# A decoder step on one core: the output projection with LN1, and the last FFN group with LN3, each ordered by token chunks

## The reference

```python
h = x @ w_in + b_in; a, g, p = jnp.split(h, [D_CONV, 2 * D_CONV], axis=-1)
u = a * jax.nn.sigmoid(g)                       # causal depthwise conv, width 31, group norm, silu
mix = jnp.concatenate([o_conv, o_pool], axis=-1) @ w_out
x = layer_norm(DN_ALPHA * x + mix, ln1_g, ln1_b)
x = layer_norm(DN_ALPHA * x + cross_attn(x, mem_k, mem_v, xq_w, xo_w), ln2_g, ln2_b)
f = jnp.square(jax.nn.relu(x @ w1 + b1)) @ w2 + b2
x = layer_norm(DN_ALPHA * x + f, ln3_g, ln3_b)
```

## Time and profile before

| | |
|---|---|
| median of 3 runs | 1454.04 us (1453.9 to 1457.93) |
| the profiled execution: its own time, its span | 1453.77 us, 1451.9 us |
| PE busy | 1374.4 us, 95% of the span, 8454 matmuls |
| DVE, POOL, ACT busy | 780.2, 671.3, 346.3 us |
| mean granted clock of PE | 0.976 |

### The profile page before, as it was taken

The page is one execution under the profiler, slowest core; times in us unless marked ns, Lnnn a source line. Parts: engine busy times, 40 slices in busy tenths (PEclk is TensorE's granted clock), DMA queues, the critical chain, the costliest instruction groups (busy, mean ns, idle before and its releaser), DMA issues.

```text
span 1451.9 us, 20585 instructions
## 1 busy us (share of the span) xinstructions
PE 1374.4 (95%) x8454; PEld 1317.0 (91%) x8454; DVE 780.2 (54%) x848; ACT 346.3 (24%) x659; POOL 671.3 (46%) x392
## 2 busy tenths in 40 slices
PE   7999889997899979999999999999999999999994
PEld 6999877696699968889999999999999999999993
DVE  4899998379712652477773115531154311454568
ACT  4222441212711431135320002200022100221114
POOL 3377986136752704539533333333333333343470
PEclk9999999998999989999999999999999999999997
DMA  8222432001011066301111111111111111111103
GB/s 249 61 48 80 120 131 73 15 29 30 15 44 44 6 230 231 129 17 37 37 44 55 47 44 44 43 44 43 45 53 48 44 44 43 44 44 45 43 15 119
DMA packets 44382, 93.52 MB, mean 64 GB/s; under 512 B 20256, under 2 KB 26656, under 8 KB 41888
## 3 DMA queue, kind: packets, MB, share of 16 engines
q1 hardware_dynamic: 34560, 89.73, 19.5%
q10 hardware_dynamic: 9760, 2.93, 0.8%
HBM read 85.39 MB, written 7.25 MB: 64 GB/s over the span
## 4 chain that ended last, share of the span: by engine, by line
PE 70%; DVE 19%; POOL 6%; issue 2%; ACT 2%; DMA 1%; SPq 0%; DVEq 0%; ACTq 0%; POOLq 0%
PE bank L589 22%; PE bank L590 21%; PE bank L591 21%; DVE conv_sum L1474 10%; POOL x_low L504 1%; DVE conv_sum L1483 1%; DVE x_full L1619 1%; ACT x_full L1270 1%; POOL x_full L349 1%; POOL w_low L340 1%; PE conv_sum L751 1%; DVE bank L1629 1%; DVE x_low L1461 1%; DMA dec_kv<-dec_kv_in 1%; DVE x_full L1636 1%
## 5 line engine op out<-in xcount | busy, mean ns | idle before, releaser
L589 PE MATMUL bank<-x_high,w_high 128*128 128x384 f32 (+1 forms) x1200 | 391.6, 326 | 15.2 <-POOL w_low L340 11.8
L338 POOL TENSOR_TENSOR w_high<-w_raw,ones 128x1024 fp32r<-128x1024 f32 x84 | 163.0, 1940 | 514.8 <-PE bank L591 255.3
L590 PE MATMUL bank<-x_low,w_high 128*128 128x384 f32 (+1 forms) x1200 | 388.6, 324 | 0.0
L591 PE MATMUL bank<-x_high,w_low 128*128 128x384 f32 (+1 forms) x1200 | 387.9, 323 | 0.0
L589 PE MATMUL bank<-mix,w_high 128*128 128x384 f32 (+1 forms) x1024 | 335.9, 328 | 7.3 <-DVE x_full L1726 2.8
L590 PE MATMUL bank<-mix,w_high 128*128 128x384 f32 (+1 forms) x1024 | 335.0, 327 | 0.0
L591 PE MATMUL bank<-mix,w_low 128*128 128x384 f32 (+1 forms) x1024 | 332.1, 324 | 0.0
L589 PEld LDWEIGHTS bank<-x_high,w_high 128*128 128x128 f32 x1200 | 226.1, 188 | 18.4 <-POOL w_low L340 11.2
L591 PEld LDWEIGHTS bank<-x_high,w_low 128*128 128x128 f32 x1200 | 226.4, 189 | 0.0
L590 PEld LDWEIGHTS bank<-x_low,w_high 128*128 128x128 f32 x1200 | 226.3, 189 | 0.0
L340 POOL TENSOR_TENSOR w_low<-w_raw,w_high 128x1024 fp32r<-128x1024 f32 x84 | 211.7, 2520 | 6.6
(11 more groups left out here) (244 smaller groups left out, 1687.7 us busy)
## 6 DMA issues: line engine op xcount, KB each, us to landing
w_raw<-slabs_in SPq DMA_DIRECT2D x110, 512.0 KB, 3.5
dec_kv<-dec_kv_in SPq DMA_DIRECT2D x16, 1024.0 KB, 5.4
scratch<-slabs_in SPq DMA_DIRECT2D x8, 512.0 KB, 3.6
yT_res<-x_full SPq DMA_DIRECT2D x4, 768.0 KB, 3.5
x_full<-xT_in SPq DMA_DIRECT2D x4, 384.0 KB, 5.1
x_full<-xT_in SPq DMA_DIRECT2D x2, 768.0 KB, 8.9
x_full<-xT_in SPq DMA_DIRECT2D x2, 576.0 KB, 10.9
yT_res<-x_full SPq DMA_DIRECT2D x2, 576.0 KB, 3.0
```

Of the source, the lines that this page charges most:

```text
L338: pool.tensor_tensor(high[:, slot, :], raw[:, p, :], one, ALU.mult).then_inc(high_done, 1)
L589: pe.matmul(out, w_high, x_high, start=first, stop=False)
L590: pe.matmul(out, w_high, x_low, start=False, stop=False)
L591: return pe.matmul(out, w_low, x_high, start=False, stop=last)
```

## The change

It has four parts. **Front**: the sample tokens' convolution is multiplied on POOL (`sample_products`) and only summed on DVE (two reductions); POOL no longer scales the window sums (ACT scales the tokens instead, `scale_tokens`, and the pool scale is divided once); DVE's `mix_low` and `e1_join` stand later between the taps; POOL makes the low halves of K and V, which DVE made; GM uses all eight PSUM banks and GT five, where each used two. **LN1**: E2 runs over chunks outermost, with all four slabs on chip (slabs 2 and 3 in `out_high`, `out_low`, their high halves made by ACT); the pivot is now the first half-depth block itself, and every later block is accumulated in PSUM with a matmul by minus 1/128 on it (`pivoted`), so that DVE needs no subtraction; LN1 of chunk c runs in steps between the joins of chunk c + 1. **Sample keys**: SP starts the first two `load_dec` before the loads of slabs 46 and 47. **LN3**: the last W2 runs over chunks outermost, with all eight down slabs on chip (`late_high`, `late_low` for six, in the place of the up products' input); joins, pivot and sums work in place on `ffn_sum`, with pivot and running sum in PSUM; the end of the last chunk is shared: POOL centres and scales two blocks, DVE six and applies gain and bias to three, ACT to five, and the output leaves in four transfers.

```diff
+LAST = NSLAB - NB
+BY_ACT, BY_DVE, BY_POOL = (0, 1, 2, 6, 7), (3, 4, 5), (6, 7)
...
+GM_BANKS, GT_BANKS = (6, 7, 0, 1, 2, 3, 4, 5), (6, 7, 3, 4, 5)
...
-        loads(S_E1 + 2, S_XO + 4)
+        loads(S_E1 + 2, S_XO + 2)
...
+        loads(S_XO + 2, S_XO + 4)
...
+                    own.done(pool.tensor_tensor(part[:, t, :, 0:TAPS], conv_dec(i)[:, :, 2 * h + t:2 * h + t + TAPS], w, ALU.mult))
...
+        pool.wait_ge(sem("k_out"), 16)
+        pool.tensor_tensor(kl[:], kf[:], kh[:].bitcast(f32), ALU.subtract).then_inc(sem("kv_low"), 1)
...
+        for n in range(S_E2 + 1, S_E2 + 4):
+            out_split_low(n)
+        squares_added(0, 1, 7)
+        squares_added(1, 1, 7)
         ln_low(1, 0, 0, 4)
-        square_sum_6(1, 2)
+        squares_added(2, 1, 3)
+        split(36, 0, 18, MEM_SLABS, freed=S_E2 + 1)
+        squares_added(2, 3, 5)
         ln_low(1, 0, 4)
-        split(37, 1, 18, MEM_SLABS)
+        split(37, 1, 18, MEM_SLABS, freed=S_E2 + 2)
+        squares_added(2, 5, 7)
         ln_low(1, 1)
...
+        splits(S_FF + 4, LAST + 2)
+        for j in range(2, NB):
+            pool.wait_ge(sem("late_w_high"), j - 1)
+            pool.tensor_tensor(late_low[:, j - 2, :], raw[:, j % 2, :], late_high[:, j - 2, :].bitcast(f32), ALU.subtract)\
+                .then_inc(split_done, 1)
...
+            if pivoted:
+                pe.wait_ge(sem("first_round"), c + 1)
+                last = pe.matmul(ps[b][:, 0:z - a], minus128[:], first_round[:, a:z], start=False, stop=True)
...
+        for c, (a, z) in enumerate(CHUNKS):
+            for turn in range(4):
+                if c == 0:
+                    pe.wait_ge(split_done, S_E2 + turn + 1)
+                slots = (wh, wl) if turn < 2 else (out_high, out_low)
+                for m in range(2):
+                    if turn == 0 and m == 1:
+                        pe.wait_ge(sem("minus_set"), 1)
+                    half_chunk("E2", turn % 2, turn, 0, m, c, PB + 1 if c == turn == m == 0 else None, slots, turn + m > 0)
+                    if turn == 0 and m == 1:
+                        b = 6 + c % 2
+                        take(b, FREED["C1"][b] + c // 2)
+                        pe.matmul(ps[b][:, 0:z - a], minus128[:], first_round[:, a:z], start=True, stop=True).then_inc(full[b], 1)
+                    if c and turn == 1 and m == 0:
+                        ln_stats(1, c - 1)
...
+        for c in range(3):
+            for j in range(NB):
+                down_chunk(j, c)
+                if j == 1:
+                    pivot_3(c)
+                    if c:
+                        stats_3(c - 1)
+        stats_3(2)
...
+            first(0)
+            square(0, 0, 3)
+            out_high_half(S_E2 + 3)
+            square(0, 3, NB)
+            for c in (1, 2):
+                first(c)
+                square(c, 0, 3)
+                mean_square(c - 1)
+                std(c - 1)
+                square(c, 3, 5 if c == 1 else NB)
+                affine(c - 1, 0)
+                if c == 1:
+                    square(c, 5, 7)
+                affine(c - 1, 1)
+                if c == 1:
+                    square(c, 7, NB)
+            mean_square(2)
...
+        late_w_high(2)
+        late_w_high(3)
+        late_w_high(4)
+        for j in range(3):
+            square_3(0, j, j + 1)
+            late_w_high(5 + j)
+        square_3(0, 3, NB)
+        for c in (1, 2):
+            square_3(c, 0, 3)
+            mean_square(c - 1)
+            std(c - 1)
+            square_3(c, 3, 6)
+            affine(c - 1, 0)
+            square_3(c, 6, NB - 1)
+            if c == 1:
+                square_3(c, 7, NB)
+            affine(c - 1, 1)
+        square_3(2, 7, NB)
+        a, z = CHUNKS[2]
+        mean_square(2)
+        act.wait_ge(sem("ln3_added"), 18)
+        act.copy(s3[:, 2, a:z], ps[2][:, 0:z - a]).then_inc(sem("tail_mean"), 1)
+        std(2)
+        act.wait_ge(sem("tail_inverted"), 1)
+        act.wait_ge(sem("ln_var"), 9)
+        act.copy(s3[:, 0, a:z], ps[5][:, 0:z - a]).then_inc(sem("tail_rstd"), 1)
+        for j in BY_ACT:
...
+            dve.wait_ge(sem("sample_products"), i + 1)
+            dve.wait_ge(sem(f"conv_out{i}"), 32)
+            out = qf[:, i, TP:T].rearrange("p (b t) -> p t b", b=SB)
+            for h in range(2):
+                ins = dve.tensor_reduce(out[:, 2 * h:2 * h + 2], sample_part(i, h), AX, ALU.add)
...
+                tt(xf[:, j, a:z], xf[:, j, a:z], ps[b][:, 0:z - a], ALU.add).then_inc(free[b], 1)
+                dve.wait_ge(free[b], FREED["E2"][b] + turn + 1)
...
+            blocks(0, 0, NB)
+            blocks(1, 0, 3)
+            variance(0)
+            centre(0, 0)
+            blocks(1, 3, 4)
+            invert(0)
+            blocks(1, 4, 5)
+            scale(0, 0)
+            blocks(1, 5, 6)
+            centre(0, 1)
+            blocks(1, 6, 7)
+            scale(0, 1)
+            blocks(1, 7, NB)
+            blocks(2, 0, 3)
+            variance(1)
+            blocks(2, 3, 4)
+            centre(1, 0)
+            blocks(2, 4, 6)
+            invert(1)
+            blocks(2, 6, NB)
+            scale(1, 0)
...
+        blocks_3(0, 0, NB)
+        for c in (1, 2):
+            blocks_3(c, 0, 3)
+            variance(c - 1)
+            centre(c - 1, 0)
+            blocks_3(c, 3, 4)
+            invert(c - 1)
+            blocks_3(c, 4, 5)
+            scale(c - 1, 0)
+            blocks_3(c, 5, 6)
+            centre(c - 1, 1)
+            blocks_3(c, 6, 7)
+            scale(c - 1, 1)
+            blocks_3(c, 7, NB)
+        a, z = CHUNKS[2]
+        n = NB - len(BY_POOL)
+        variance(2)
+        dve.wait_ge(sem("tail_mean"), 1)
+        own.done(tt(acc[:, 0:n, a:z], acc[:, 0:n, a:z], over_blocks(ps[2][:, 0:z - a], n), ALU.subtract))
+        invert(2)
+        dve.sem_inc(sem("tail_inverted"), 1)
+        dve.wait_ge(sem("tail_rstd"), 1)
+        for j in range(0, n, 2):
+            x2 = acc[:, j:j + 2, a:z]
+            tt(x2, x2, over_blocks(ps[5][:, 0:z - a], 2), ALU.mult).then_inc(sem("ln_scaled"), 1)
+        for j in BY_DVE:
+            dve.wait_ge(sem("ln_scaled"), 32 + j // 2 + 1)
+            ts(acc[:, j, a:z], acc[:, j, a:z], col("ln3_g", j), col("ln3_b", j), ALU.mult, ALU.add).then_inc(sem("y_by_dve"), 1)
```

594 lines of the change are left out of this document (344 added, 250 removed).

## The result

The changed kernel takes 1414.99 us, the median of 4 runs (1413.90 to 1416.35); beside it the kernel before took 1455.99 (1453.90 to 1458.17). The ratio is 0.9719, 95% interval 0.9698 to 0.974. Forecast were 1409.5 us and a range of 1398 to 1424. The profiled execution is the longest of the four, 1416.35 us; its span is 37.4 us shorter than the one of before, whose execution was the shortest of its kind.

What follows compares the result with a forecast made beforehand. PE is busy 1374.4 of 1451.9 us, so only its waits and low-clock time can be won. Gains of 12.2 + 14.1 + 8.8 + 9.3 = 44.4 us give 1409.5 us, range 1398 to 1424.

Steps and rivals of the forecast that it cites:

- Part A: Front up to E2: no wait ahead of the means, shorter GM and GT; gain 12.2 us (bounds 3.5 and 13.8).
- I take 5.3: most of GT is over before the clock drops: GT and the half slab behind it gain 5.3 us; at full clock 6.9, at half speed over all GT a 3.4 loss.
- The term for GM: Group norm's means take 7.5 us on eight banks instead of 11.2: gain 3.7, less 0.5 for E1's third slab.
- Part B: E2, LN1 and XQ's first pair take 91.5 us, waits included, instead of 105.6: gain 14.1 (bounds 2 and 23).
- Part C: Sample keys issued earlier: the 6.7 us wait goes, half-speed work behind it shrinks by 2.1; gain 8.8 (bounds 6 and 9.3).
- Part E: Last group: 2.1 us from PE's content, 7.2 behind the last product (17.1 against 24.3); gain 9.3 (bounds 4 and 12).
- that of the statistics: Behind PE's last product, the last statistics were given 0.5 us of the 17.1 us tail.
- (1): LN1 keeps its stalls, through later handovers or the low clock: Part B gives 4 instead of 14, 1419.5 us; chance 18%.
- (2): All waits hide, GT and E2 keep the clock: A 13.8, B 20, E 10, 1401 us; chance 10%.
- (3): Last group's late slabs not double buffered in effect: 7.4 instead of 4.2 us for six slabs, 1428.5 us; chance 6%.
- (4): Short waits in E2 pull the clock to 1.2 GHz over E2 and XQ's pair: slower, 1490 us; chance 3%.
- any wait for `split_done` in the last group: Sign of a wrong forecast: PE waiting for a slab's split in the last group, where late slabs were to be hidden.

Runs made afterwards that it cites:

- spread_128_rows: Changed kernel with GT's twelve spreading matmuls over 128 rows instead of 24, the added rows of the selecting matrix zero: 1409.89 us, ratio 0.9690.
- filled: Changed kernel with unread matmuls added, 24 ahead of E2's wait for chunk 2's copy and 12 ahead of LN3's last statistics: 1413.01 us, ratio 0.9728.
- copy_ahead: Changed kernel with chunk 1's last square and the copy of chunk 2's first block ahead of affine(0, 1) on ACT in LN1: 1413.26 us, ratio 0.9718.
- squares_ahead: Kernel of copy_ahead with chunk 2's last two sums of squares ahead of slab 37's split on POOL in LN1: 1411.63 us, ratio 0.9719.

## Why the prediction was right, and where it was off

**What bounds the kernel.** Right: PE's content stayed, and all of the gain came out of its waits and its clock. Content at 0.161 us a matmul, with the waits added, foretold E2's stage to 1.3 us and the last group to 0.8.

**Part A**, 12.2 forecast, 8.1 measured in this pair of executions. The failed step is "I take 5.3: most of GT is over before the clock drops". The low level began 4.6 us into GT, with half of it over, lasted 10.2 us and took in most of the half slab as well: 2.3 us came from GT (with two banks GT is again at 11.86) and 0.1 from the half slab, 2.4 in place of 5.3. The forecast saw the cause, matmuls with 24 rows which stay, and then took a value near the wrong end; `spread_128_rows` shows another 5.1 us that were there to win. The term for GM was right in size (2.95 measured between the means' start and the next slab, 3.7 less 0.5 forecast) by luck, for its cause was the clock and not the banks: eight banks give 0.35 at full clock, and the kernel before lost the rest by its low clock. What pulled that down is not settled. The wait ahead of the means went, as forecast, because of two reductions of 0.64 us, but the first mean came only 2.7 us earlier where 3.7 were forecast: E1 had a low stretch in its first 6 us, worth 1.5 us, which the second profile of the changed kernel does not have. That the reductions now hold E1 up by 1.2 us, the forecast did not say.

**Part B**, 14.1 forecast, 12.85 measured, a stage of 92.8 us where 91.5 was foretold; other profiles have up to 94.0. This is the part that the order of instructions on five engines decides, and the walk through it held: PE at the copy's matmul 43.3 us behind E2's start (42.8), the copy ready at 47.7 (46.5), wait 4.44 (3.8), PE at the third statistics at 68.0 (64.7), the last sum at 70.4 (66.8), wait 2.46 (2.1), slab 38's slot 1.47 (1.3). The low clock behind the first wait is there: 0.71 over 5.84 us costs 1.7 us, for 2 forecast, and `filled` removes it. `copy_ahead` and `squares_ahead` show that both waits have the causes named. The joins and running sums of the new stage lasted 0.45 to 0.57 us, one of them 0.67, where the earlier trace rows has one of 2.13: priced as operations on PSUM, they came out right. The taps, which also read PSUM, took 1.29 us, beside the products that moved to POOL too, as they did in the kernel before.

**Part C**, 8.8 forecast, 8.6 measured, 8.5 by undoing it in the profiles and 9.9 in the medians, which are from two chips. Right in full: the keys' wait is gone (1.5 us are left, the slot's), and the clock of the stretch is 1.00 where it was 0.60.

**Part E**, 9.3 forecast, 7.85 in this pair. (The forecast's own 102.2 less 99.9 is 2.3; its sum takes 2.1.) The six late slabs never stop PE: in either `raw` slot POOL's low parts start 7.3 to 7.6 us apart, where 7.4, or 3.7 a slab, was forecast. Groups of POOL in the last group (count, busy us, mean ns, idle before):

```profile
L641 POOL TENSOR_TENSOR w_late_low<-w_raw,w_late_high 128x1024 fp32r<-128x1024 f32 x6 | 14.8, 2463 | 7.3 <-ACT w_late_high L1615 7.2
```

Products and statistics took 100.68 us for 99.9. Behind the last product 17.97 for 17.1: the last join, with the operation behind it, ends 2.57 us behind it (3.0), and from the last variance to the end it is 11.65 (12.0), but the eight statistics matmuls took 3.81 us at clock 0.57 and end 2.5 us behind ACT's last square, where 0.5 was forecast; in `filled`, at full clock, they took 2.17 us and end 0.9 behind it. The other profiles with this end have 16.4 to 17.3 us behind the last product, so the forecast's 17.1 lies among them, and the mis-sized term is that of the statistics.

**The rivals.** (1), LN1 keeps its stalls, and (2), all hides, bracket the truth; B's 12.85 is close to the forecast. (3), late slabs not double buffered, is refuted by the row above. The only wait of PE in the last down products is 0.48 us at 1300.71, for the split of the second slab, which is not one of the six. The prediction named any wait for `split_done` in the last group as a sign that it is wrong; this one costs 0.48 us and bears on neither its path nor its size. (4), the half clock in E2 through short waits, did not come: the stage has a pivot matmul that waits on another engine behind every half block, and its clock is 0.98. The Trainium skill (TensorE: Matmul & The Clock Gate, "A second HAM failure mode: psum-queue depth-cycling") describes an engine that swings between its clocks through such pauses; this trace does not show it. The same page says under "Why this matters for your kernels" that a single matmul with 32 rows takes the time of one with 128. In time alone the rows agree: GT's first four matmul instructions took 1.55 us with 24 rows and, in `spread_128_rows`, 1.45 with 128 (first row and second). The clock was 1.00 in both; what came on top was its fall behind them.

```profile
274.38 1.55 PE L831 MATMUL conv_sum<-scratch,gn_select 24*128 24x384 f32 x4
```

```profile
274.46 1.45 PE L831 MATMUL conv_sum<-scratch,gn_select 128*128 128x384 f32 x4
```

**Medians.** The forecast was made against one execution of before. The measured gain is 41.0 us by the medians, 37.4 by the two profiles, since the changed kernel's profile caught the longest of four and that of before the shortest. By medians, 3.4 of 44.4 us are missing. The medians do not say where; GT and its half slab, 2.9 us short in this pair, are the likeliest place.

## What to carry to other kernels

A run of matmuls with few rows costs its time once and may cost the clock of what follows it: 10 us of it here. Padding the stationary matrix with rows of zeros took no time here, where the other operand's buffer already had 128 rows. When one order puts an instruction behind eight others on its engine, and an engine that bounds the kernel waits for it, move it, and then look for the wait that comes next on the next engine: here ACT's order was worth 1.6 us or more and uncovered POOL's, and the low clock moved to the next wait too. A stage's content per matmul and a walk through every queue foretold the reordered stage within 1.4% in one profile and 2.7% in the worst; what they don't foretell is the clock.

## What was not expected of the hardware

- Twelve matmuls with 24 rows, issued without a gap, and the half slab of 128-row matmuls behind them ran at a mean clock of 0.74 and 0.69; with 128 rows, 104 of them zero in the selecting matrix, at 1.00 (9.81 and 8.23 us against 6.89 and 6.01). So it was in all eleven profiles with 24 rows and all three with 128.
- The clock's answer to a wait differs from place to place and, at some places, from run to run. Behind the 1.9 us wait ahead of E1 it fell in five of nine profiles, behind the wait of 2.2 to 2.6 us ahead of the last statistics in five of eleven; ahead of the means it fell in a wait of 3.4 us (the kernel before) and stayed up through one of 3.2. In E2 it fell behind the wait of 4.1 to 4.4 us in eight of eight and, where that wait was 2.1 us, in none of three, but then behind the next wait of 2.7 to 3.8 us. Such a fall costs about 1.5 to 3 us on top of the wait (0.72 over 6 us, 0.50 over 5.84).
- Matmuls that nobody reads kept the clock up where a wait had lowered it, without shortening the wait: 1.00 for 0.71 over 5.8 us in E2, and 1.00 for 0.72 behind the wait for slab 37.
